# A fused transformer kernel: how the operands of its last down projection are prepared

## The reference

```
ff = (silu(hn @ w_gate) * (hn @ w_up)) @ w_down      # 1024 -> 2816 -> 1024
h = h + rmsnorm(ff, post_ffn_norm)
e = rmsnorm(p @ w_ple_proj, ple_norm)
h = h + e * sigmoid(h @ w_ple_gate + b_ple_gate)
```

## Time and profile before

| | us |
|---|---|
| median of 3 runs | 1532.63 |
| lowest, highest | 1531.97, 1532.64 |
| the profiled execution: its time | 1534.16 |
| its span | 1532.4 |
| TensorE busy | 1512.4 |
| DVE busy | 1193.8 |
| ACT busy | 813.0 |
| POOL busy | 133.8 |

### The profile page before, as it was taken

How to read it: one execution, slowest core, us unless ns; L and a number is a source line. 1 busy time by engine, 2 the same in 40 slices (tenths; PEclk the granted TensorE clock), 3 DMA queues, 4 the chain that set the end, 5 groups by cost and what they waited for, 6 DMA issues and landing times.

```text
span 1532.4 us, 22218 instructions
## 1 busy us (share of the span) xinstructions
PE 1512.4 (99%) x8502; PEld 1301.7 (85%) x8502; DVE 1193.8 (78%) x1911; ACT 813.0 (53%) x1296; POOL 133.8 (9%) x141
## 2 busy tenths in 40 slices
PE   8999999999999999999999999999999999999998
PEld 4788877878888899999888888888888999988987
DVE  8989997897898789987573547766488888878877
ACT  5535467754553656666433336456365656554443
POOL 0111000000000101111021011100202100000010
PEclk9999999999999999999999999999999999999999
DMA  9678221223566447656623323111343444436451
GB/s 370 171 185 200 97 90 62 79 94 104 212 231 210 165 121 192 193 157 165 187 95 104 110 86 118 62 42 42 110 139 126 133 133 134 129 104 192 111 185 69
DMA packets 64908, 211.01 MB, mean 138 GB/s; under 512 B 7581, under 2 KB 9885, under 8 KB 63778
## 3 DMA queue, kind: packets, MB, share of 16 engines
q1 hardware_dynamic: 52784, 178.63, 34.1%
q0 software_dynamic: 12016, 30.95, 10.3%
q10 hardware_dynamic: 2, 0.00, 0.0%
HBM read 175.47 MB, written 7.87 MB: 120 GB/s over the span
## 4 chain that ended last, share of the span: by engine, by line
PE 88%; DVE 6%; ACT 3%; issue 2%; DMA 1%; ACTq 0%; DVEq 0%
PE bank L2144 15%; PE bank L2152 15%; PE bank L2145 15%; PE bank L2182 8%; PE bank L2192 8%; PE bank L2184 8%; PE bank L2256 2%; PE bank L2269 1%; PE bank L2268 1%; PE bank L2270 1%; PE bank L2228 1%; PE bank L2238 1%; PE bank L2229 1%; PE bank L2360 1%; PE bank L2343 1%
## 5 line engine op out<-in xcount | busy, mean ns | idle before, releaser
L2144 PE MATMUL bank<-HH,sph 128*128 128x512 f32 x856 | 342.9, 401 | 2.5 <-ACT HH L2774 0.9
L2145 PE MATMUL bank<-HH,spl 128*128 128x512 f32 x856 | 333.8, 390 | 0.0
L2813 DVE TENSOR_TENSOR spl<-raw,sph 128x1024 fp32r<-128x1024 f32 (+1 forms) x150 | 183.2, 1223 | 112.1 <-ACT sph L2420 112.0
L2152 PE MATMUL bank<-HL,sph 128*128 128x512 f32 x856 | 225.5, 396 | 0.0
L2420 ACT ACTIVATE sph<-raw 128x1024 fp32r<-128x1024 f32 (+2 forms) x170 | 172.3, 1017 | 99.4 <-PE bank L2152 63.3
L2144 PEld LDWEIGHTS bank<-HH,sph 128*128 128x128 f32 x856 | 160.8, 188 | 40.5 <-issue 6.0
L2145 PEld LDWEIGHTS bank<-HH,spl 128*128 128x128 f32 x856 | 160.8, 188 | 34.5 <-issue 1.4
L2152 PEld LDWEIGHTS bank<-HL,sph 128*128 128x128 f32 x856 | 159.8, 188 | 35.2 <-issue 1.9
L2875 DVE SCALAR_TENSOR_TENSOR convout<-convin,vecs,convout 128x512 f32<-128x512 f32 x240 | 166.3, 743 | 0.0
L2182 PE MATMUL bank<-HH,sph 128*128 128x256 f32 x576 | 144.6, 283 | 0.1
L2184 PE MATMUL bank<-HH,spl 128*128 128x256 f32 x576 | 144.4, 283 | 0.0
(11 more groups left out here) (410 smaller groups left out, 2947.8 us busy)
## 6 DMA issues: line engine op xcount, KB each, us to landing
raw<-in_w_in SPq DMA_DIRECT2D x69, 512.0 KB, 3.3
raw<-in_w_up SPq DMA_DIRECT2D x66, 512.0 KB, 4.1
more<-in_w_ada SPq DMA_DIRECT2D x32, 512.0 KB, 5.5
raw<-in_w_down SPq DMA_DIRECT2D x28, 512.0 KB, 3.7
raw<-in_w_gate SPq DMA_DIRECT2D x22, 512.0 KB, 3.5
raw<-raw POOLq DMA_DIRECT2D x36, 256.0 KB, 4.2
spl<-raw POOLq DMA_DIRECT2D x17, 512.0 KB, 5.6
ada<-in_w_ada SPq DMA_DIRECT2D x16, 512.0 KB, 11.3
```

Source lines behind the costliest of these rows:

```text
L2144: e.matmul(P_[b][:], sph(n)[:, q], hi[:, k, :], start=k == 0, stop=False)
L2145: e.matmul(P_[b][:], spl(n)[:, q], hi[:, k, :], start=False, stop=False)
L2152: m = e.matmul(P_[b][:], sph(n)[:, q], low[:, k, :], start=False, stop=last and k == kb - 1)
L2813: e.tensor_tensor(spl(n), raw(n), sph(n).bitcast(F32), ALU.subtract).then_inc(*up("s_w_low", ("wl", n)))
```

## The change

1. `sevens` gets a hook `then`. In the last tile of the second up stage it emits activation sums: `down_t_sum(0,0)` in part total-3, its high half in total-2, `down_t_sum(0,1)` in total-1, its high half after the gate eviction, `down_t_sum(1,0)` after silu, `down_t_sum(1,1)` and the high half of (1,0) after the mid copy. To have room, `DH[0]` and `DS[0]` stand in XT's place, and the output accumulates in `FFO`; the residual comes back into `XT`.
2. All weights' sums stand in `bsum`, each emitted a part earlier, behind `down_low` of the part before; `down_third` likewise.
3. The plain units cut during the plain stage (2 to 7) take the way "dma".
4. Tail: the square of the last tile in two pieces by ACT, one earlier; column sums behind the first embedding product; the w_pg unit in the fourth slot of the ring is unit 0, not 1; three units cut by DVE before the end, one by POOL.

```diff
@@ down_factors
             pos = s % 7
-            if pos in (2, 3):
-                add("down_sum", s)
             add("down_high", s)
             if beside:
                 beside()
                 beside = None
             add("down_low", s)
             st["made"] += 1
-            if pos in (2, 4, 5) or pos == 6 and s < st["total"] - 1:
+            if pos in (1, 2):
+                add("down_sum", s + 1)
+            if pos in (1, 3, 4) or pos == 5 and s < st["total"] - 7:
                 load()
-            if pos == 6 and s < st["total"] - 1:
-                add("down_sum", s + 2)
+            if pos == 5 and s < st["total"] - 7:
+                add("down_sum", s + 3)
                 add("down_third", s // 7 + 1)
@@ sevens
+            if then:
+                then(s - total)
             add("seven", which, s, sum_bank(i), pair_bank(i))
...
         for pos in range(6):
             settle(pos, i)
+            if then:
+                then(pos)
@@ second FFN
+    def sums_of_down(s):
+        if s in (-3, -1):
+            add("down_t_sum", 0, (s + 3) // 2, [])
+        elif s in (-2, 0):
+            add("down_t_high", 0, (s + 2) // 2)
+        elif s == 2:
+            add("down_t_sum", 1, 0, [])
+        elif s == 4:
+            add("down_t_sum", 1, 1, [])
+            add("down_t_high", 1, 0)
...
     def down_first():
-        t_sums(0)
-        yield
-        t_sums(1)
-        yield
+        held = [label for j in range(4) for label in frees[j]]
+        add("down_t_high", 1, 1)
         add("down_t_low", 0, 0)
         yield
         add("down_t_low", 0, 1)
         yield
-        t_sums(3)
-        yield
-        add("down_t_low", 1, 0)
-        add("down_t_low", 1, 1)
+        for g in range(2):
+            add("down_t_sum", 3, g, held)
         yield
         for g in range(2):
-            add("down_x_low", 0, g)
+            add("down_t_high", 3, g)
+        add("down_t_low", 1, 0)
         yield
-        for g in range(2):
-            add("down_t_sum", 2, g, [])
+        add("down_t_low", 1, 1)
+        add("down_t_sum", 2, 0, [])
+        yield
+        add("down_t_sum", 2, 1, [])
+        yield
+        add("down_x_low", 0, 0)
+        yield
+        add("down_x_low", 0, 1)
         yield
         add("down_sum", 1)
         add("down_third", 0)
...
+    lo_engine[0] = "dma"
     load()
     side.append(down_first())
@@ seven-part stage
     def down_square(s):
         p, pos = divmod(s, 7)
-        if pos in (5, 6):
+        if p == 3 and pos in (4, 6):
+            add("last_square", pos)
+        elif pos in (5, 6):
             i = 2 * p + pos - 5
-            ssf.add(("XT", i), [("ff", i)], last=i == 7)
+            ssf.add(("FFO", i), [("ff", i)])
...
-        if s >= DOWN_PARTS - 2:
+        for _ in range({DOWN_PARTS - 2: 2, DOWN_PARTS - 1: 1}.get(s, 0)):
             split()
@@ tail
-    b = ssf.columns()
-    root = rsqrt("ff", ssf.sums(b), T, 1.0 / D, [("cols", "ff")], eps_row)
...
         add("hl", be, "p2", n_last, (i - 6) * 256, 0, 2, bfree)
-        if i == 6:
+        if i == 7:
             row = spread("ff", ("small", root), [("rs", "ff")])
...
+        if i == 6:
+            b = ssf.columns()
+            root = rsqrt("ff", ssf.sums(b), T, 1.0 / D, [("cols", "ff")], eps_row)
@@ program
-        fourth = [n for n in range(len(units)) if units[n][0:2] in (("w_gate", 0), ("w_pg", 1))]
+        fourth = [n for n in range(len(units)) if units[n][0:2] in (("w_gate", 0), ("w_pg", 0))]
...
+            def last_square(pos):
+                w.wait_ge(at("down_low", DOWN_PARTS - 4), at("down_add", 3, pos))
+                q = slice(256, 512) if pos == 4 else slice(0, 256)
+                labels = [("sq", "ff", 7)] if pos == 6 else []
+                e.activation(TMP[NT][:, q], FFO[:, 7, q], ACT.Square).then_inc(*up("s_square", *labels))
```

More of the change, by code:

```diff
@@ L1001, in sevens, with ffn_up @@
         main.give(sum_bank(i)[0], ("seven_mid", which, i))
-    def ffn_up(which, acts, names, hook=None):
+    def ffn_up(which, acts, names, hook=None, then=None):
         jobs = []
@@ L1650, in plan @@
         held_e.append((be, g))
+        if i == 6:
+            b = ssf.columns()
+            root = rsqrt("ff", ssf.sums(b), T, 1.0 / D, [("cols", "ff")], eps_row)
+            misc.give(b, ("rs", "ff"))
     done()
@@ L1739, in program @@
         tmp_at = o
-        TMP = [place(f"tmp{i}", o + 2048 * i, [128, S]) for i in range(NT)]; o += 2048 * NT
+        TMP = [place(f"tmp{i}", o + 2048 * i, [128, S]) for i in range(NT)] + [place("tmp_last", last_at, [128, S])]
+        o += 2048 * NT
         o += -(base + o) % 512
@@ L1755, in program @@
         TS.append(place("ts3", B + 36864, [128, 4, 256]))
-        DH = [[place(f"dh{t}{g}", 16384 * (1 + t) + 8192 * g, [128, 4, 256], F32R)[:] for g in range(2)] for t in range(2)]
-        DL = [[place(f"dl{t}{g}", 16384 * (1 + t) + 8192 * g + 4096, [128, 4, 256], F32R)[:] for g in range(2)]
+        DH = [[place(f"dh{t}{g}", 32768 * t + 8192 * g, [128, 4, 256], F32R)[:] for g in range(2)] for t in range(2)]
+        DL = [[place(f"dl{t}{g}", 32768 * t + 8192 * g + 4096, [128, 4, 256], F32R)[:] for g in range(2)]
               for t in range(2)]
-        DS = [[place(f"ds{t}{g}", 16384 * (1 + t) + 8192 * g + 4096, [128, 4, 256])[:] for g in range(2)]
+        DS = [[place(f"ds{t}{g}", 32768 * t + 8192 * g + 4096, [128, 4, 256])[:] for g in range(2)]
               for t in range(2)]
@@ L2632, in down_plain @@
                 w.wait_ge(at("tile", g), *fenced("d2"))
-                e.activation(XT[:, i, :], P_[b][:], ACT.Copy).then_inc(*up("s_branch_a", ("down_plain", i)))
+                e.activation(FFO[:, i, :], P_[b][:], ACT.Copy).then_inc(*up("s_branch_a", ("down_plain", i)))
             def down_t_high(t, g):
-                w.wait_ge(at("down_t_sum", t, g), *fenced("d2"))
+                w.wait_ge(at("down_t_sum", t, g), *down_place(t, g))
                 if t == 2:
@@ L3162, in down_t_sum @@
                 first, second = slice(0, 256), slice(256, 512)
-                w.wait_ge(*[at("seven_mid", 2, f - SEVEN[2][0]) for f in range(k0.start, k1.stop)], *fenced("d2"),
-                          *each(free))
+                w.wait_ge(*[at("seven_mid", 2, f - SEVEN[2][0]) for f in range((k1 if t == 1 else k0).start,
+                                                                              (k0 if t == 0 else k1).stop)],
+                          *down_place(t, g), *each(free))
                 to = DS[t][g]
@@ L3198, in down_sum @@
                     if s > 7:
-                        w.wait_ge(at("down_low", s - 6), at("down_sum", s - 5))
+                        w.wait_ge(at("down_low", s - 5))
                     ins = e.tensor_tensor(BSUM[:], raw(down_raw(s, 1)), raw(down_raw(s, 2)), ALU.add)
-                elif pos == 2:
-                    n = down_raw(s, 0)
+                else:
+                    n = down_raw(s, {2: 0, 3: 3}[pos])
                     w.wait_ge(at("raw", n), at("down_low", s - 1))
                     ins = e.tensor_tensor(BSUM[:], BSUM[:], raw(n), ALU.add)
[L3205 to L3208, removed]
                 ins.then_inc(*up("s_w_low", ("down_sum", s)))
@@ L3223, in down_add @@
                 last = {5: [("ff", i)], 6: [("ff", i)]}.get(pos, [])
-                e.tensor_tensor(XT[:, i, cols], XT[:, i, cols], bank, ALU.subtract if i % 2 else ALU.add).then_inc(
+                e.tensor_tensor(FFO[:, i, cols], FFO[:, i, cols], bank, ALU.subtract if i % 2 else ALU.add).then_inc(
                     *up("s_branch", ("down_add", p, pos), *last))
@@ L3558, in x_reload @@
                 w.wait_ge(*[at("x_spilt", which, i) for i in range(8)])
-                to = FFO if which == 2 else XT
-                e.dma_start(to[:, 4 * half:4 * half + 4, :], A["x_scratch"][:, 4 * half:4 * half + 4, :]).then_inc(
+                e.dma_start(XT[:, 4 * half:4 * half + 4, :], A["x_scratch"][:, 4 * half:4 * half + 4, :]).then_inc(
                     *G.up(f"d_xb{half}", ("x_back", which, half), by=16))
```

30 lines of the change are left out of this document (14 added, 16 removed).

## The result

The changed kernel takes 1538.60 us (median of 5 runs, 1537.97 to 1540.53) beside 1532.50 for the kernel before in the same comparison: a ratio of 1.0041, 95% interval [1.0029, 1.0053], slower by 6.1 us. The profiled execution took 1538.6 (span 1536.8); that of before took 1534.16.

What follows compares the result with a forecast made beforehand. TensorE was taken as the bound, so only its waits could be won back. Plain stage +7.0 (0.85 from the up stage within it), clock +2.9, seven-part stage -4.8, tail -1.1: +4.0, median 1536.6 us, range 1530.0 to 1540.4.

Steps and rivals of the forecast that it cites:

- Sums in the up stage: Last tile of the up stage: the first sum delays seven_up and TensorE's last part, 0.85 us lost.
- Unit 2's transfer: Plain stage: unit 2's low half lands at 1366.3, wanted at 1361.35, so TensorE waits 5.0 us.
- rival of short transfers: Plain stage: 384 KB adding transfers land in some 3.2 us, no second wait, -4.4 without a clock fall; chance 0.12.
- Later units hidden: Plain stage: units 3 to 6 hidden with 1.1 us to spare, costing only if a transfer takes over 5.5 us.
- POOL's queue: Plain stage: unit 7's transfer stands behind the weights' third in POOL's program, a second wait of 4.1 us before tile 7.
- The clock: Plain stage: granted clock falls in both long waits, costing 1.7 us for the first and 1.2 for the second, +2.9.
- the 1.7 taken from the tail: Cost of one clock fall, read from the earlier kernel after 1473.75: 3.4 us at half speed cost 1.7.
- the 3.4 that I gave the rule: Both plain-stage waits: by the skill's throttle rule the clock falls in each, 3.4 us in the sum, 0.5 more.
- Seven-part stage: Seven-part stage: sums a part earlier and DVE ahead let the 28 parts run at their 80.6 us, -4.8.
- Tail: Tail: first join addition 0.69 instead of 2.10 us, last square shorter, last additions later; -1.1, between 0 and -1.7.
- clock kept up: Rival for the plain-stage waits: clock stays up in one or both, +2.8 or +1.1; chance 0.28.
- Slow transfers: Rival for the plain stage: adding transfers land in 5.9 us and later units wait, +8 to +10; chance 0.10.

Runs made afterwards that it cites:

- run 9: Run 7 with both activation sums of the first part put behind the last up part's evictions: 1525.09 us, ratio 0.9954.
- run 3: Changed kernel with the adding transfer of the weights' third emitted two steps later, behind unit 7's split: 1534.41 us, ratio 1.0013.
- run 4: Changed kernel with sixteen idle 512-column matmuls ahead of plain tile 2: 1545.14 us, ratio 1.0085.
- run 7: Run 1 with the weights' second sum and its third emitted two steps later: 1525.65 us, ratio 0.9953.
- run 8: Run 7 with the activations' sums put back from the up stage into the down stage: 1530.08 us, ratio 0.9983.
- run 2: Kernel before with only the low halves of plain units 2 to 7 made by adding transfer: 1537.62 us, ratio 1.0036.
- run 12: Run 9's kernel measured again, unchanged, beside run 11: 1523.86 us, ratio 0.9949.
- run 10: Run 9 with the low half of plain unit 7 alone made by copy and adding transfer: 1525.76 us, ratio 0.9954.
- run 1: Changed kernel with the low halves of plain units 2 to 7 made by DVE again: 1528.49 us, ratio 0.9974.
- run 11: Run 9 with two idle 512-column matmuls ahead of the joined half's first product: 1524.03 us, ratio 0.9946.
- run 5: Changed kernel with four idle 512-column matmuls ahead of plain tile 2: 1536.99 us, ratio 1.0027.
- run 6: Changed kernel with unit 2 also split by DVE and the weights' third behind unit 7's split: 1532.1 us over 10 runs, ratio 0.9994.

## Why the prediction was right, and where its sizes were off

Forecast +4.0 within -2.6 to +7.8, slower at 0.58; measured +6.1. The mechanism was as forecast: both long waits, in their places, with both falls of the clock. By its steps:

- *Sums in the up stage, +0.85.* The last part waited 0.58 us and started 0.74 behind the rhythm; with its slow restart tile 0 came 0.84 late. Run 9 takes the wait away by moving the sum. Right.
- *Unit 2's transfer, a wait of 5.0.* The chain was worked to an issue 8.65 us after tile 0's start (1353.2 to 1361.85); it came 8.74 after (1350.95 to 1359.69). Landing was taken as 4.4 and was 3.8, and tile 2 was wanted 0.2 later, so the wait was 4.20. Mechanism right, 0.8 too much. The rival of short transfers needed 3.3.
- *Later units hidden up to a landing of 5.5.* The bound was right, the cover was not there: unit 6's landing took 7.4 (issued at 1377.22, tile 6 starts at 1384.71), beside the two loads that unit 5's landing had set free. **A third wait of 1.88 us, in no term of the sum.** That two of my terms (loads and transfer) fall on each other's time was said only of unit 7.
- *POOL's queue, a wait of 4.1 ahead of tile 7.* Measured 4.11, but partly by luck. From unit 5's landing to unit 7's the forecast had 13.3 us and the trace shows about 15.7, because the extra load took 7.0 and not 4.7; tile 7 was wanted 2.4 later as well, most of it by the third wait (1.88). The two misses cancel. (The working's own terms also add up to +20.3 where it has +20.4.) Run 3 shows the order in the queue as the cause.
- *The clock, +2.9.* Measured 2.8 and 1.7, together 4.5. The first fall cost 1.1 more than the 1.7 taken from the tail: it lasted 5.7 us of work. This is the largest miss of a single term. The 1.7 itself was read roughly: idle and one-column matmuls fill the tail of before only to 1476.6, and a microsecond of 512-column products runs at full clock before the fall at about 1477.6. By the Trainium skill's rule (TensorE: Matmul & The Clock Gate, Part 1), activity releases the throttle. The trace agrees in sign: the clock goes to 0.50 at about 1362.5, within the wait ahead of tile 2, and at about 1393.2, as tile 7 starts behind its wait. By the 3.4 that I gave the rule, 1.1 was still missing. That it stayed up behind 1.88 us, and in run 4 behind 2.68, my sum did not have: it took every long wait for a fall.
- *Seven-part stage, -4.8.* Measured 80.96 us without a wait, -4.5. The size was right, the reason is shown in part. With everything but the transfers (and the second sum later) the stage takes 82.0, 3.5 less than before (runs 7 and 9, table below), but 86.0 where the activations' sums go back as well (run 8). So it is DVE's lead on entering the stage that counts, and the earlier weights' sums alone gain nothing there. The transfers with the old order of the sums give 3.0 (run 2, 82.6), and without tile 7's wait the stage takes 82.7 (run 3): part of the gain rests on the waits of the plain stage, in which DVE gets ahead. DVE's idle of 0.85 us ahead of a low half is still there at 1404.48 and 1421.27 and shrinks to 0.26 only from 1425 on. The single buffer is not tested apart from the earlier sums.
- *Tail, -1.1.* Measured -1.8, just past the lower end I gave. The slow addition went as forecast, and in this profile the clock stayed up, which it did not before; how the 1.8 divides between the two no run shows. By runs 9 and 12 the clock can be kept or lost in the same kernel: in runs 7 to 10 it falls behind this wait, and the stretch from there to the end takes 51.2 us instead of 49.6.

Sum: +0.8 +12.1 -4.5 -1.8 = +6.6 where it was 0.85 +6.15 +2.9 -4.8 -1.1 = +4.0. The step that failed in size is the plain stage, by some 3: 1.9 for the third wait, 1.6 for the clock, less 0.8 for the first transfer, and 0.4 of small restarts. The rivals: clock kept up is out by the stretches at 0.50, short transfers by the 3.8 of unit 2's, which no landing of the 23 that go this way undercuts (their median is 5.5). Its own numbers were loose too: with 3.2 in place of 4.4 and 5.3 the chain to unit 7 adds up to +17.0 and not +16.1, still a wait of 0.7. Slow transfers (+8 to +10) was nearer than its 0.10 suggests, since of the three behind 1370 the median was 5.8. The range ended at +7.8, just short of it.

The lengths of the stages by run, in us, from the profiles (marks as in the earlier trace rows):

| | plain | seven-part | low halves of units 2 to 7 |
|---|---|---|---|
| before | 35.92 | 85.5 | DVE |
| changed | 48.02 | 81.0 | transfer |
| run 1 | 33.65 | 84.7 | DVE |
| run 2 | 44.12 | 82.6 | transfer, old order of the sums |
| run 3 | 41.99 | 82.7 | transfer, third behind unit 7's |
| run 7 | 33.49 | 82.0 | DVE, second sum later |
| run 8 | 34.31 | 86.0 | DVE, second sum later, activations' sums back |
| run 9 | 33.24 | 82.0 | DVE, second sum later, first two sums a part later |

What the change is worth without the transfers: run 1 gives -4.0; with the second sum later, run 7, -6.8; with the first two sums later as well, runs 9 and 12 together, -7.5. The six transfers, meant to relieve DVE, took work from an engine for which the stage waited 2.4 us and gave it to a path for which it waited 10.2.

## What to carry to other kernels

A difference of 0.95 us on a loaded engine is not replaced by a copy and a transfer of 4 to 7.5 us unless the slack of each tile, counted from its load's landing to its use, is longer than that; count it unit by unit. Look at what stands ahead of each moved transfer in its issuer's queue, and at which loads its landing sets free, since those loads then run beside the next transfer. Relief for a busy engine is better found in an earlier stage where it idles (4.4 us here), and in not letting it stand at a load with work behind it (2.8 us here).

## What the runs showed of the hardware

- *An idle's length alone does not settle the clock.* In run 4's profile it fell behind a wait of 1.81 us and stayed at 1.00 behind one of 2.68, 9 us later. In the tail TensorE waits 1.85 us in every kernel with the changed tail except run 11. The changed kernel's profile has the clock at 1.00 behind it and 49.6 us from there to the end of the span; run 9's has 0.50 and 51.2 us; run 12, the same program, has 1.00 and 49.6. Run 12's five times stand in two groups, 1523.83 to 1523.86 and 1525.71 to 1525.86, as such a fall would make them, but only one of the five is profiled and run 9's five show no such groups. Idles of 1.94 us in runs 1 and 6 were followed by half clock, idles of 1.88 (changed kernel) and 1.74 (run 3) were not.
- *Idle matmuls do not always hold it.* In run 5 they did. In run 11 the clock fell 1.5 us before them, while TensorE ran 512- and 128-column products behind two groups of one-column ones, and was at 0.50 while they ran. Why there is open.
- *A plain float32 matmul of 512 columns* is shown as two instructions and takes 0.9 us (3.60 for four), where a product on rounded halves starts 0.23 us after the one before.
- *Adding transfers and loads that run together take longer.* 384 KB within the SBUF landed in 3.8 us with nothing beside it (unit 2) and in 7.4 beside two loads of 512 KB (unit 6); one of these loads took 7.0 where 4.7 is the median of before. Unit 7's, issued behind another adding transfer of 512 KB, took 5.8.
- *One kernel's times scatter far more than the others'.* Run 6, with five adding transfers, has 6.3 us between the ends of its ten times, run 1 with none 2.0. But run 2 with six has 1.2 (five times) and run 9 with none 3.2 (five times), so the transfers are not shown as the cause.
